# Norm statistics with tokens on partitions, one modulation slice ahead of the sums, GpSimd's sample tiles in another order, in a two-layer retention and attention trunk

## Chip, cores and metric

The kernel runs on one core of a Trainium2 chip. The metric is the device time of one execution in microseconds. A core has five engines that run side by side and meet at semaphores: TensorE (matrix products into PSUM), VectorE, ScalarE, GpSimd and SyncE, which here issues the loads of the weights.

## What is computed

Two layers of a hybrid encoder trunk, for a prompt (1 x 256 tokens) and for 8 sequences of 16 new tokens, 384 tokens in all, width 1024, fp32:

```python
mods = silu(c) @ w_ada + b_ada
sh1, sc1, g1, sh2, sc2, g2 = split(mods, 6)                 # per sequence
h  = rmsnorm(x, g_mix) * (1 + sc1) + sh1
u  = h @ w_in            # retention q, k, v, gate | attention q, k, v | two merge gates
x  = x + g1 * ((sig(m_r) * yA @ w_br_ret + sig(m_a) * yB @ w_br_att) @ w_out)
h2 = rmsnorm(x, g_ffn) * (1 + sc2) + sh2
x  = x + g2 * (relu(h2 @ w_up)**2 @ w_down)
rmsnorm(x, g) = x * rsqrt(mean(x * x over the 1024 features) + 1e-6) * g
```

yA is an eight-head retention, yB an attention over a band of chunks and a cache. The change is in `rmsnorm` and what stands around it.

## The kernel before

x is kept transposed, `xT[feature within tile, 8 feature tiles, 384 tokens]`: features lie on the partitions, so a sum over features is a sum across partitions, which TensorE does. Every large product is made of three passes on split operands (high times high, low times high, high times low; `hhi`/`hlo` for activations, `whi`/`wlo` for weights), and weight blocks of 128x1024 pass through four raw slots and two split slots: SyncE loads, ScalarE writes `whi` (`high`), VectorE writes `wlo` (`low`).

Each layer runs: norm, value product, eight heads, merge, output product, norm, up product, down product. The norm of layer 0's mixing takes its statistics from x before it is transposed (`first_tables`, `spread`) and isn't touched. The three others go through the same functions, and the order on each engine is written out by hand:

- ScalarE squares the feature tiles two at a time into `sq` (L802). GpSimd adds the first six into `sq_sum` (L430, L434); the last two stay in `sq`.
- TensorE, `norm` (L1635): with `ones` as the stationary operand it sums `sq_sum` (L1641) and the two `sq` tiles (L1644) over the partitions. Bank X0 then holds, on every partition, the sum of each of the 384 tokens.
- ScalarE, L815: square root of these 384 columns into `std`. VectorE, `inverse_std` (L1151): reciprocals of `std` into `rstd`, first the 128 sample columns (L1153), then the 256 prompt columns (L1154).
- Prompt part: VectorE scales tile k by `modA` and `rstd` into `hp` (L1164), ScalarE adds the shift and rounds into `hhi` (L827), VectorE forms `hlo` (L1169). Sample part: GpSimd, `norm_sample` (L637), multiplies by `modA` (L643), by `rstd` (L649) and adds the shift (L653); ScalarE rounds into `hhi` (L772), VectorE forms `hlo` (L1174). VectorE's order is `normed_tiles` (L1176): tile m's low parts come behind the scaling of tile m+2.
- TensorE meanwhile computes slices of the modulation (`silu(c) @ w_ada`, 512 columns each) for later use with stationary operands of 32 columns (L1650): `last_modulation` (L1833) in the norm ahead of the up product, three slices in layer 0 and two in layer 1, into X1, X2, X3; `ada_products` (L1655) in layer 1's mixing norm, the last of which writes X0.
- `steady` (L1877) and the end of `last_modulation` are dummies, products of `ones` with `ident` into a bank that nobody reads.
- The first product after the norm is `first_up` (L1847, matmuls on L1861) or the value product (L1627); each starts a tile when its `hlo` is there.

## Time and profile before

| | us |
|---|---|
| median of 3 runs | 1806.72 (1802.99 to 1807.86) |
| the profiled execution's own time | 1803.19 |
| its span | 1801.2 |
| TensorE busy in it | 1782.5 |
| VectorE, ScalarE, GpSimd busy | 994.8, 736.0, 353.4 |

The profiled execution lies 3.5 us below the median of the runs. Times in the rows are microseconds from the start of the span. A matmul on fp32 operands shows as two records, each with a weight load of its own (PEld); one on fp32r operands or a transpose shows as one. "x192" is a number of records merged into one row, whose time is from the first's start to the last's end.

### The profile page before, as it was taken

How to read it: one execution, taken by the hardware profiler on the slowest of the kernel's cores; microseconds unless marked ns; L12 is line 12 of the kernel's file. 1: busy time of each engine (PE TensorE's matmuls, PEld its weight loads, DVE VectorE, ACT ScalarE, POOL GpSimd, SP SyncE). 2: the span in 40 equal slices, each digit the busy share in tenths (PEclk: the TensorE clock that was granted, in tenths of full speed). 3: DMA queues.
4: the chain of work that ended last, by engine and by line, in shares of the span. 5: the costliest groups of instructions: out<-in, count | busy, mean ns of one | idle time of the engine just before them, and what ended most of it. 6: DMA issues, size and time to landing. Idle time of an engine off the chain costs nothing.

```text
span 1801.2 us, 35393 instructions
## 1 busy us (share of the span) xinstructions
PE 1782.5 (99%) x11933; PEld 1624.8 (90%) x11933; DVE 994.8 (55%) x1606; ACT 736.0 (41%) x1411; POOL 353.4 (20%) x459
## 2 busy tenths in 40 slices
PE   8999999999999999999999999999999999999998
PEld 7888888889999999999988888888899999999998
DVE  5466666667433575543364666666674346655333
ACT  3444444446222344532234444444463234554222
POOL 3333333330000120000023334333300004000000
PEclk9999999999999999999999999999999999999999
DMA  9878898896666734455638779888865635344432
GB/s 343 232 200 215 225 239 231 231 236 199 210 211 208 260 95 127 129 177 200 218 104 237 204 215 230 231 224 240 231 220 165 211 118 199 117 128 125 132 125 99
DMA packets 505240, 348.47 MB, mean 193 GB/s; under 512 B 201931, under 2 KB 468109, under 8 KB 505110
## 3 DMA queue, kind: packets, MB, share of 16 engines
q1 hardware_dynamic: 484992, 292.13, 56.3%
q0 software_dynamic: 12592, 44.99, 7.7%
q10 hardware_dynamic: 7526, 9.58, 1.5%
q8 instruction: 86, 1.41, 0.3%
q14 instruction: 44, 0.36, 0.1%
HBM read 313.56 MB, written 34.37 MB: 193 GB/s over the span
## 4 chain that ended last, share of the span: by engine, by line
PE 97%; DVE 1%; ACT 1%; issue 1%; ACTq 0%; POOL 0%; DVEq 0%
PE G L1591 50%; PE G L1627 32%; PE X L1752 8%; PE X L1650 2%; PE X L1551 2%; PE G L1861 2%; PE X L1627 1%; DVE wlo L1093 0%; PE X L1644 0%; DVE hp L1164 0%; DVE rstd L1154 0%; ACT hp L791 0%; ACTq L766 0%; ACT whi L772 0%; DVE hlo L1169 0%
## 5 line engine op out<-in xcount | busy, mean ns | idle before, releaser
L1093 DVE TENSOR_TENSOR wlo<-raw,whi 128x1024 fp32r<-128x1024 f32 x369 | 471.0, 1277 | 546.0 <-ACT whi L772 543.9
L772 ACT ACTIVATE whi<-raw 128x1024 fp32r<-128x1024 f32 x369 | 390.9, 1059 | 761.8 <-PE G L1591 442.3
L1627 PE MATMUL G<-whi,hhi 128*128 128x512 f32 x832 | 333.9, 401 | 1.7 <-DVE hlo L1169 1.4
L1627 PE MATMUL G<-whi,hlo 128*128 128x512 f32 x832 | 325.0, 391 | 0.0
L1627 PE MATMUL G<-wlo,hhi 128*128 128x512 f32 x832 | 324.5, 390 | 0.1
L1591 PE MATMUL G<-hhi,whi 128*128 128x384 f32 x704 | 236.8, 336 | 0.0
L1591 PE MATMUL G<-hhi,wlo 128*128 128x384 f32 x704 | 235.4, 334 | 0.0
L1591 PE MATMUL G<-hlo,whi 128*128 128x384 f32 x704 | 235.3, 334 | 0.0
L1627 PEld LDWEIGHTS G<-whi,hhi 128*128 128x128 f32 x832 | 156.2, 188 | 49.2 <-issue 13.1
L1591 PE MATMUL G<-ysp,whi 128*128 128x384 f32 x768 | 196.9, 337 | 0.0
L1627 PEld LDWEIGHTS G<-wlo,hhi 128*128 128x128 f32 x832 | 156.1, 188 | 34.1 <-DVE wlo L1093 0.6
L1627 PEld LDWEIGHTS G<-whi,hlo 128*128 128x128 f32 x832 | 156.4, 188 | 29.4
L1591 PE MATMUL G<-fhi,whi 128*128 128x384 f32 x512 | 172.5, 337 | 0.0
L1591 PE MATMUL G<-fhi,wlo 128*128 128x384 f32 x512 | 172.1, 336 | 0.0
L1591 PE MATMUL G<-flo,whi 128*128 128x384 f32 x512 | 172.1, 336 | 0.0
L1591 PEld LDWEIGHTS G<-ysp,whi 128*128 128x128 f32 x768 | 138.4, 188 | 1.5 <-issue 1.2
L1591 PEld LDWEIGHTS G<-hhi,whi 128*128 128x128 f32 x704 | 132.1, 188 | 2.8 <-issue 1.6
L430 POOL TENSOR_TENSOR sq_sum<-sq 128x384 f32<-128x384 f32 x4 | 5.1, 1286 | 655.4 <-ACT sq L802 655.4
L1591 PEld LDWEIGHTS G<-hlo,whi 128*128 128x128 f32 x704 | 132.2, 188 | 0.1
L1591 PEld LDWEIGHTS G<-hhi,wlo 128*128 128x128 f32 x704 | 132.1, 188 | 0.0
L1591 PE MATMUL G<-ysp,wlo 128*128 128x384 f32 x384 | 129.2, 336 | 0.0
L1591 PEld LDWEIGHTS G<-fhi,whi 128*128 128x128 f32 x512 | 96.1, 188 | 0.6 <-issue 0.6
(237 smaller groups left out, 2545.3 us busy)
## 6 DMA issues: line engine op xcount, KB each, us to landing
raw<-in_w_in_dram SPq DMA_DIRECT2D x256, 128.0 KB
raw<-in_w_in_dram SPq DMA_DIRECT2D x128, 256.0 KB
raw<-in_w_up_dram SPq DMA_DIRECT2D x64, 512.0 KB
raw<-in_w_down_dram SPq DMA_DIRECT2D x64, 512.0 KB
raw<-in_w_in_dram SPq DMA_DIRECT2D x49, 512.0 KB
ada_w<-in_w_ada_dram SPq DMA_DIRECT2D x44, 512.0 KB, 6.1
kc<-in_cache_attn_k_dram SPq DMA_DIRECT2D x64, 256.0 KB, 6.7
vc<-in_cache_attn_v_dram SPq DMA_DIRECT2D x32, 512.0 KB, 7.5
```

Source lines behind the costliest of these rows:

```text
L430: ops.tensor_tensor(sq_sum[:, :], sq[:, 0, :], sq[:, 1, :], ALU.add).then_inc(sq_used, 2)
L772: return a.activation(out, in_, ACT.Copy)
L1093: v.tensor_tensor(wlo[:, j % SPLIT, :, :], raw[:, j % RAW, :, :], whi[:, j % SPLIT, :, :].bitcast(F32), ALU.subtract).then_inc(blk_split, 1)
L1551: return t.transpose(out, in_, ident[0:k, 0:k])
L1591: ins = t.matmul(G[b][:, 0:TOK], w[:, s, k, n * P:(n + 1) * P], x[:, k0 + k, :], start=first and k == 0 and x is hi and w is whi, stop=las ...
L1627: ins = t.matmul(B[banks[m][0]][:, :], x[:, kp * WK + k, m * P:(m + 1) * P], w[:, k, :], start=first and k == 0 and x is hhi and w is w_hi ...
L1650: ins = t.matmul(x[32 * g:32 * g + 32, 0:P], cT[:, k, :], part, start=start, stop=stop, skip_group_check=True)
L1752: return t.matmul(out, lhsT, rhs, start=start, stop=stop, skip_group_check=True)
L1861: ins = t.matmul(G[b][:, 0:TOK], w[:, j % SPLIT, k % BK, n * P:(n + 1) * P], x[:, k, :], start=k == 0 and x is hhi and w is whi, stop=k == ...
```

## The change

It does five things. (1) In `norm` on TensorE the squares become the stationary operand and a column of `ones` the moving one: nine one-column matmuls put the sum of token p of tile n on partition p, column 384 + n, of X0; a tenth, over columns of `qr_par` that are always zero, opens the three columns. (2) ScalarE's root and VectorE's reciprocal work on three columns; VectorE lays the result out as three diagonal matrices (`std_diag`), TensorE multiplies them with `ones` (`std_spread`), which again puts each token's value on every partition, and VectorE copies X0 into `rstd`. (3) One slice of the modulation is issued ahead of `norm` instead of behind it, and in layer 1's mixing norm the remaining one waits for the copies out of X0. Layer 1 has four dummies fewer. (4) GpSimd multiplies four sample tiles by `modA` ahead of its wait for `rstd` and the other four between the later steps. (5) VectorE forms the first tile's low parts ahead of the third tile's scaling.

```diff
--- before.py
+++ after.py
@@ -223,7 +223,7 @@
     band = sb("band", [DEPTH * HEADS, BAND], stack=xstack)
     hp = sb("hp", [P, NS, PR], stack=xstack)
     hs = sb("hs", [P, KT, P], stack=xstack)
-    std = sb("std", [P, TOK], stack=xstack)
+    std_diag = sb("std_diag", [P, NT, P], stack=xstack)
     rstd = sb("rstd", [P, TOK], stack=xstack)
     x_diag = sb("x_diag", [P, NT, P], stack=xstack)
     x_ss = sb("x_ss", [P, 4], stack=xstack)
@@ -639,19 +639,38 @@
 
             pool.wait_ge(res_ready, c.norm * KT + R0)
             pool.wait_ge(moda_ready, c.norm * 4 + 4)
-            for k in range(KT):
+            scaled, normal = {}, {}
+
+            def scale(k):
                 c.op(g.tensor_tensor(seqs(hs[:, k, :]), seqs(xT[:, k, PR:TOK]),
                                      modA[:, k, 1:NSEQ].unsqueeze(2).to_broadcast([P, SB, ST]), ALU.mult))
-            c.settle()
+                scaled[k] = c.now["own"] + c.mine
+
+            def normalize(k):
+                pool.wait_ge(pool_own, scaled[k])
+                c.op(g.tensor_tensor(hs[:, k, :], hs[:, k, :], rstd[:, PR:TOK], ALU.mult))
+                normal[k] = c.now["own"] + c.mine
+
+            def shifted(k):
+                pool.wait_ge(pool_own, normal[k])
+                d = seqs(hs[:, k, :])
+                g.tensor_tensor(d, d, modT[:, shift * KT + k, 1:NSEQ].unsqueeze(2).to_broadcast([P, SB, ST]),
+                                ALU.add).then_inc(hs_ready, 1)
+
+            for k in range(KT // 2):
+                scale(k)
             pool.wait_ge(rstd_ready, c.norm * 2 + 1)
-            for k in range(KT + 1):
-                if k < KT:
-                    c.op(g.tensor_tensor(hs[:, k, :], hs[:, k, :], rstd[:, PR:TOK], ALU.mult))
-                if k:
-                    pool.wait_ge(pool_own, c.now["own"] + (c.mine - 1 if k < KT else c.mine))
-                    d = seqs(hs[:, k - 1, :])
-                    g.tensor_tensor(d, d, modT[:, shift * KT + k - 1, 1:NSEQ].unsqueeze(2).to_broadcast([P, SB, ST]),
-                                    ALU.add).then_inc(hs_ready, 1)
+            normalize(0)
+            shifted(0)
+            normalize(1)
+            for k in range(KT // 2, KT):
+                scale(k)
+                shifted(k - 3)
+                normalize(k - 2)
+            for k in range(KT - 3, KT - 1):
+                shifted(k)
+                normalize(k + 1)
+            shifted(KT - 1)
 
         def store_prompt_state(c, l, h):
             pool.wait_ge(stp_ev, c.head)
@@ -812,7 +831,7 @@
                 high(c, 1)
                 square(c, KT - 2)
                 act.wait_ge(sq_used, c.norm * KT + KT)
-                a.activation(std[:, :], X[0][:, 0:TOK], ACT.Sqrt, scale=1.0 / DM, bias=eps_t[:, 0:1]).then_inc(std_ready, 1)
+                a.activation(rstd[:, 0:NT], X[0][:, TOK:TOK + NT], ACT.Sqrt, scale=1.0 / DM, bias=eps_t[:, 0:1]).then_inc(std_ready, 1)
             for k in range(KT):
                 if first and k in (2, 4, 6):
                     if k > 2:
@@ -1150,8 +1169,13 @@
 
         def inverse_std(c):
             dve.wait_ge(std_ready, c.norm + 1)
-            v.reciprocal(rstd[:, PR:TOK], std[:, PR:TOK]).then_inc(rstd_ready, 1)
-            v.reciprocal(rstd[:, 0:PR], std[:, 0:PR]).then_inc(rstd_ready, 1)
+            c.op(v.reciprocal(rstd[:, 4:4 + NT], rstd[:, 0:NT]))
+            c.settle()
+            v.tensor_tensor(std_diag[:, :, :], ident[:, :].unsqueeze(1).to_broadcast([P, NT, P]),
+                            rstd[:, 4:4 + NT].unsqueeze(2).to_broadcast([P, NT, P]), ALU.mult).then_inc(diag_ready, 1)
+            dve.wait_ge(spread_done, c.norm + 1)
+            v.tensor_copy(rstd[:, PR:TOK], X[0][:, PR:TOK]).then_inc(rstd_ready, 1)
+            v.tensor_copy(rstd[:, 0:PR], X[0][:, 0:PR]).then_inc(rstd_ready, 1)
 
         def modulated(c, shift, gain, k0, k1):
 
@@ -1175,20 +1199,24 @@
 
         def normed_tiles(c, shift, k0, k1, block=None, at=None, free=None):
 
+            def tile_low(m):
+                dve.wait_ge(hhi_ready, c.norm * KT + (m + 1))
+                if m == k0 and free is not None:
+                    dve.wait_ge(ada_used, free)
+                c.op(sample_low(m))
+                prompt_low(shift, m).then_inc(h_ready, 1)
+
             for k in range(k0, k1 + 2):
                 if k == (k1 if at is None else at) and block is not None:
                     low(c, block)
+                if k == k0 + 2:
+                    tile_low(k0)
                 if k < k1:
                     if k >= NS:
                         dve.wait_ge(h_ready, c.norm * KT + (k - NS + 1 + H0))
                     scaled(k)
-                if k >= k0 + 2:
-                    m = k - 2
-                    dve.wait_ge(hhi_ready, c.norm * KT + (m + 1))
-                    if m == k0 and free is not None:
-                        dve.wait_ge(ada_used, free)
-                    c.op(sample_low(m))
-                    prompt_low(shift, m).then_inc(h_ready, 1)
+                if k > k0 + 2:
+                    tile_low(k - 2)
 
         def first_modulation(c, part):
 
@@ -1635,13 +1663,24 @@
         def norm(c):
 
 
-            pe.wait_ge(std_ready, c.norm)
+            pe.wait_ge(rstd_ready, c.norm * 2)
             pe.wait_ge(pair_ev, c.head * 4 + P0)
             pe.wait_ge(sq_used, c.norm * KT + KT - 2)
-            t.matmul(X[0][:, 0:TOK], ones[:, :], sq_sum[:, :], start=True, stop=False)
-            for n in range(2):
-                pe.wait_ge(sq_ready, c.norm * KT + (KT - 1 + n))
-                t.matmul(X[0][:, 0:TOK], ones[:, :], sq[:, n, :], start=False, stop=(n == 1)).then_inc(sq_used, 1)
+            mm(X[0][:, TOK:TOK + NT], ones[:, :], qr_par[:, 0, ST:ST + NT], stop=False)
+            for n in range(NT):
+                mm(X[0][:, TOK + n:TOK + n + 1], sq_sum[:, n * P:(n + 1) * P], ones[:, 0:1], start=False, stop=False)
+            for k in range(2):
+                pe.wait_ge(sq_ready, c.norm * KT + (KT - 1 + k))
+                for n in range(NT):
+                    ins = mm(X[0][:, TOK + n:TOK + n + 1], sq[:, k, n * P:(n + 1) * P], ones[:, 0:1], start=False, stop=(k == 1))
+                ins.then_inc(sq_used, 1)
+
+        def std_spread(c):
+
+            pe.wait_ge(diag_ready, c.norm + 1)
+            for n in range(NT):
+                ins = mm(X[0][:, n * P:(n + 1) * P], ones[:, :], std_diag[:, n, :])
+            ins.then_inc(spread_done, 1)
 
         def ada_product(x, k, w, start, stop, blocks=True):
 
@@ -1830,15 +1869,12 @@
                         ada_products(mixed(l, 20 * i + j))
                         j += 1
 
-        def last_modulation(l):
-
-            for f in range(ADA_F + 1 - l):
-                pe.wait_ge(adaf_full[f], l * 32 + 32)
-                for k in range(KT):
-                    ins = ada_product(X[1 + f], k, adaf_w[:, f, k, :], k == 0, k == KT - 1)
-                ins.then_inc(ada_mm, 1)
-            for _ in range(8 * l):
-                mm(X[3][:, 0:P], ones[:, :], ident[:, :])
+        def last_modulation(l, f):
+
+            pe.wait_ge(adaf_full[f], l * 32 + 32)
+            for k in range(KT):
+                ins = ada_product(X[1 + f], k, adaf_w[:, f, k, :], k == 0, k == KT - 1)
+            ins.then_inc(ada_mm, 1)
 
         def up(c):
             for j in range(4):
@@ -1911,9 +1947,10 @@
         for l in range(DEPTH):
             if l:
                 with cnt.turn({"norm": 1}, use=("norm", "head")) as c:
+                    ada_products(ADA_GAP)
                     norm(c)
-                    ada_products(ADA_GAP)
-                    pe.wait_ge(std_ready, c.norm + 1)
+                    std_spread(c)
+                    pe.wait_ge(rstd_ready, c.norm * 2 + 2)
                     ada_products(ADA_GAP + 1)
                 steady(4)
             with cnt.turn(S_V.adds, also=("norm",)) as c:
@@ -1936,8 +1973,14 @@
                     pe.wait_ge(m_ready, c.mix + j % 2 * BK)
                     products(c, S_OUT, j, S_OUT.groups[j // 2], mhi, mlo, j % 2 * BK, j % 2 == 0, j % 2 == 1)
             with cnt.turn({"norm": 1}, use=("norm", "head")) as c:
+                pe.wait_ge(pair_ev, c.head * 4 + P0)
+                last_modulation(l, 0)
                 norm(c)
-            last_modulation(l)
+                std_spread(c)
+            for f in range(1, ADA_F + 1 - l):
+                last_modulation(l, f)
+            for _ in range(4 * l):
+                mm(X[3][:, 0:P], ones[:, :], ident[:, :])
             with cnt.turn(S_UP0.adds, also=("norm",)) as c:
                 first_up(c)
             with pe.Fori(0, S_UP.turns - 1) as i, cnt.turn(S_UP.adds) as c:
```

## Rows read from the trace of the kernel before

**Rows 1.** The page's first part: busy time, share of the span, instructions.
```profile
PE 1782.5 (99%) x11933; PEld 1624.8 (90%) x11933; DVE 994.8 (55%) x1606; ACT 736.0 (41%) x1411; POOL 353.4 (20%) x459
```

**Rows 2.** What TensorE waited for: total us, times, longest.
```profile
PE X L1644 <- ACT sq L802: 2.7, 3, 0.9
...
PE G L1861 <- DVE wlo L1093: 0.8, 2, 0.4
```

**Rows 3.** The chain that ended last, layer 0, feed-forward norm: start, us, what.
```profile
629.95 1.57 PE X L1644 x4
...
631.55 0.59 ACT std L815
...
634.87 0.48 DVE hp L1164
...
636.57 0.49 DVE hlo L1174
```

**Rows 4.** Timeline of the same norm: start, us, engine, line, [idle before, releaser].
```profile
628.23 0.81 PE L1641 MATMUL X<-sq_sum,ones 128*128 128x384 f32 x2
...
629.39 1.05 ACT L802 ACTIVATE sq<-xT 128x384 f32<-128x384 f32 x2
...
631.44 5.45 PE L1650 MATMUL X<-adaf_w,cT 128*32 128x128 f32 x192
...
635.95 0.29 ACT L772 ACTIVATE hhi<-hs 128x128 fp32r<-128x128 f32 x1
...
637.71 0.45 PE L1861 MATMUL G<-hhi,whi 128*128 128x384 f32 x1 [0.82 <-DVE hlo L1169]
```

**Rows 5.** Timeline of layer 1's mixing norm, TensorE.
```profile
912.02 0.81 PE L1641 MATMUL X<-sq_sum,ones 128*128 128x384 f32 x2
...
918.86 1.16 PE L1752 MATMUL X<-ident,ones 128*128 128x128 f32 x8
...
921.40 0.50 PE L1627 MATMUL G<-whi,hhi 128*128 128x512 f32 x1 [1.38 <-DVE hlo L1169]
```

**Rows 6.** Timeline of layer 1's feed-forward norm, TensorE.
```profile
1516.15 0.81 PE L1641 MATMUL X<-sq_sum,ones 128*128 128x384 f32 x2
...
1525.60 0.44 PE L1861 MATMUL G<-hhi,whi 128*128 128x384 f32 x1 [0.56 <-DVE hlo L1169]
```

**Rows 7.** Loads of `adaf_w`, both layers: ns of issue, first and last start.
```profile
L543 SPq DMA_DIRECT2D adaf_w<-in_w_ada_dram x8: 372/490/1223, 597.4 to 1494.5; - x8
...
DMA to landing us min/median/max: 5.1/9.2/12.1
```

**Rows 8.** Timeline of the program's start, TensorE: narrow transposes, dummies.
```profile
9.97 0.66 PE L1551 MATMUL G<-ident,csil 9*128 9x9 f32 x8 [0.43 <-ACT csil L795]
...
20.21 1.06 PE L1752 MATMUL X<-ident,ones 128*128 128x128 f32 x8
```

**Rows 9.** Weight loads by line, min/median/max ns, first and last start.
```profile
L1551 PEld LDWEIGHTS G<-ident,csil x8: 133/136/138, 10.0 to 10.4; 9*128 9x128 f32 x8
...
L1641 PEld LDWEIGHTS X<-sq_sum,ones x6: 188/188/189, 628.1 to 1516.1; 128*128 128x128 f32 x6
...
L1650 PEld LDWEIGHTS X<-adaf_w,cT x320: 106/110/110, 631.4 to 1522.7; 128*32 128x32 f32 x160
```

**Rows 10.** Small operations: timeline rows, then groups (busy us, mean ns of one).
```profile
626.64 0.20 ACT L811 ACTIVATE warm<-eps_t 128x1 f32<-128x1 f32 x1
...
13.40 0.56 DVE L1124 TENSOR_TENSOR x_diag<-ident,x_rs 128x384 f32<-128x384 f32 x1 [0.35 <-POOL x_rs L613]
...
L1387 DVE RECIPROCAL small<-small 128x3 f32<-128x3 f32 x16 | 2.7, 168 | 0.0
...
L1145 DVE COPY ada_s<-X 128x128 f32<-128x128 f32 x20 | 5.7, 283 | 0.0
...
L649 POOL TENSOR_TENSOR hs<-hs,rstd 128x128 f32<-128x128 f32 x24 | 13.2, 555 | 0.5 <-POOL hs L643 0.5
```

**Rows 11.** Stretches: us, busy (instructions) by engine, granted clock, DMA share, GB/s.
```profile
12.10:19.00 6.90, 6.23 (x65) 5.52 (x67) 1.93 (x7) 2.21 (x4) 2.45 (x4) 0.51 1.08 366
...
912.00:921.40 9.40, 7.11 (x145) 5.29 (x143) 7.77 (x13) 4.48 (x10) 7.58 (x16) 1.00 0.34 108
```

## The prediction

> **What bounds the kernel now.** I read the page first. TensorE is busy 99% of the span [rows 1]. So only two things can move the end: TensorE's own work, and the few places where it stands still. The list of what TensorE waited for [rows 2] and the timeline [rows 4 to 6] name them. Apart from the start of the program the largest are the squares of the last two feature tiles (2.7 us in three waits) and the first normalized tile (0.82 and 0.56 us before the two up products, 1.38 us before the value product). All lie in the three norms that the change edits: feed-forward norm of layer 0 (A), mixing norm of layer 1 (B), feed-forward norm of layer 1 (C). The norm of layer 0's mixing is a separate code path and is not touched.
>
> The chain of waits through A gives the anatomy [rows 3]. The sums end at 631.5; I call this moment T, where bank X0 holds the sums. Then ScalarE takes the root of 384 columns (0.59), VectorE inverts as many, the first scaled tile starts at 634.87 = T+3.36, and TensorE's first real product starts at 637.71 [rows 4], 2.84 us after that. Meanwhile TensorE does something useful: 192 records of three modulation slices, 5.45 us [rows 4], so one slice (64 records) is 1.82 us. The whole stop from 628.23 to 637.71 is 9.5 us, and B (912.02 to 921.40) and C (1516.15 to 1525.60) are 9.4 and 9.5 us [rows 5, 6]. In A the old sums' first record starts at 628.23, 3.28 before T; B and C have the same steps, so T is 915.3 and 1519.43 there.
>
> **Part 1, the slice in front of the sums.** In A and C one of the modulation slices, in B the slice that stood between the sums and the wait for the root, is issued before the sums. The work is the same, 1.82 us; it fills the time in which TensorE waited for the squares. Its weights landed long before: the latest of the loads named in [rows 7] is issued at 1494.5, over 21 us ahead of the sums in C, and lands within 12.1; in A and B they are earlier still. A change from products over all 128 columns to slices over 32 costs about 0.2 us: the dummies start 0.2 us after the last slice record [rows 5]. In A the slice runs from 628.43 to 630.25 and the sums may start at 630.45. The last square is finished at 630.44 (629.39 plus 1.05) [rows 4]. So until here nothing is lost: TensorE arrives just as the data does. But nothing of the sums has been done by then either, whereas before the part over `sq_sum` was already finished (628.23 plus 0.81). All ten matmuls of the new sums now stand behind T's last input.
>
> **Part 2, the sums with tokens on partitions.** Before: three matmuls of 384 columns, two records each. After: ten matmuls (one that opens three columns, three over `sq_sum`, two times three over `sq`), each with a new 128x128 fp32 stationary operand and one to three moving columns, 20 records. Moving columns cost nothing; the weight load is what is left. The trace of before has no such matmul, so I bound it. From below: eight transposes of 9 rows, one record each, take 0.66 us in all, 0.202 the last, so 0.065 apart [rows 8]. From above: dummies of 128 fp32 columns, 8 records in 1.06 us, 0.113 apart [rows 8]. Between them decides the duration of a load: 0.188 for 128 columns of fp32, 0.110 for 32 columns, 0.136 for the 9-row transposes [rows 9]. 96 more columns cost 0.078 us, so 128 columns occupy the load path for 0.104 us, and a load that isn't a transpose costs more than the transposes' one. I take 0.11 per record: 0.1 for the first load, 19 x 0.11 and 0.2 for the last matmul, 2.39 us. New T in A is 630.45 + 2.39 = 632.84, 1.33 later than before. In B: 912.2 + 1.82 + 0.2 + 2.39 = 916.6 against 915.3. In C: 1516.35 + 1.82 + 0.2 + 2.39 = 1520.76 against 1519.43. With 0.065 per record the sums take 1.54 and T is 0.45 to 0.5 later.
>
> The Trainium skill prices this otherwise: its page "TensorEngine Tiling (Array Packing)", section "Instruction Overhead", gives each matmul about 60 cycles of overhead whatever its few columns, which at 2.4 GHz is an estimated 25 ns. By that alone the 20 records would take 0.5 us and the whole change would come out at about 2.3 us faster. The load rows above speak against it, since none of them is that short for 128 columns.
>
> **Part 3, root, inverse and spreading.** From T on: ScalarE starts 0.04 later, root of three columns 0.2 (a one-column ScalarE instruction [rows 10]); VectorE inverts three columns in 0.168 [rows 10], hand-overs 0.02 before and 0.15 after it; `std_diag` is the same instruction as `x_diag` at the program's start, 0.56 [rows 10]; TensorE starts 0.05 later and spreads with six records: 5 x 0.113 + 0.27 = 0.84; VectorE copies 128 and 256 columns out, 0.1 + 0.28 [rows 10] + about 0.35 = 0.73; 0.13 to the first scaled tile. Sum 2.89 against 3.36: 0.47 saved. The wait for the spread stands in VectorE's queue; behind it are only the copies and the scaled tiles, which need it anyway. GpSimd waits for the same sum.
>
> **Part 4, order of the tiles.** VectorE takes the low part of the first tile before it scales the third. Before, the third scaled tile kept it until 636.57 although ScalarE had the sample part at 635.95 + 0.29 = 636.24 [rows 3, 4]: 0.27 gained. First tile ready to TensorE: T + 2.89 + 2.84 - 0.27 = T+5.46. The second tile then comes 0.5 us later relative to the first (two scaled tiles in front), about 2.1 us behind it, which is what TensorE needs for one tile's six matmuls over both groups (12 x 0.17): no stall. GpSimd's new order does tile 0 first and puts the four remaining modulated copies between the others: at some 0.55 us per instruction [rows 10] tile 1 is ready at T+5.1, tile 3 at T+8.2, before VectorE comes to them (its own pace is 1.55 us per tile). No cost, no gain.
>
> **Part 5, TensorE's own path after the spread.** The spread's last record is issued at T+1.76, the next slice may start at about T+2.0. A: two slices 3.63 + 0.2: first product at T+5.83, later than the tile (T+5.46), so TensorE's work decides. A = 632.84 + 5.83 = 638.67, against 637.71: **+0.96**. C: one slice and four dummies (fewer by four, 0.9 us less work) end near T+4.9, so the tile decides: 1520.76 + 5.46 = 1526.22 against 1525.60: **+0.62**. B: here the remaining slice writes X0 and now waits for both copies out of it, T+2.76: 2.81 + 1.79 + 0.2 + four dummies 0.95 = T+5.75, so the work decides: 916.61 + 5.75 = 922.36 against 921.40: **+0.96**. Sum +2.5 us. With the lower price of the sums it is +0.1, +0.1 and -0.2, together 0.0.
>
> What is late next: nothing else moves with it. In A and C a wait of 0.4 us for the low half of the third weight block follows eight steps later; that block waits for TensorE to free a slot, so the wait travels along.
>
> **The forecast.** Against the profiled execution's own time, 1803.19 (span 1801.2 and 2.0 around it), +2.5 gives 1805.7. The three runs shown have a median of 1806.72 and lie between 1802.99 and 1807.86; on the median's footing it is **1809.2 us**. About 0.3% (5.4 us) is what a measurement of this kernel can tell from no change, so this is no change.
>
> **Rivals.** (1) *Narrow matmuls are cheap.* At 0.065 per record the sum is 0.0: 1806.7. For it: the transposes. Against: the load rows. (2) *The clock falls*, the slower case. Before, the granted clock is full through all three norms, yet near the start it fell to half (1.2 of 2.4 GHz) at about 12.1 and stayed there until about 19, after a spell of eight 9-column transposes with gaps on either side [rows 8, 11]. That is like the new stretch: 2.4 us of one-column matmuls, then 1.2 us of standing still for the root and the diagonal, before only half such gaps. Price: of 6.85 us at half clock some 1.5 are waits anyway, the other 5.35 lose half, 2.7 us per norm. One fall gives 1806.7 + 2.5 + 2.7 = 1811.9, all three 1817.3. It decides from two falls on (1814.6), and one lies at the border of 0.3%. The page "TensorE: Matmul & The Clock Gate" of the Trainium skill, section "A second HAM failure mode: psum-queue depth-cycling", says that short idle times between groups of matmuls are enough to make the clock swing; by it this rival would be the rule, though the gaps of 0.9 and 0.8 us in the norms of before did not do it. Against it too: slices and dummies stand on both sides. (3) *A gain*: loads go in ahead under the slice, and little is left after the last square. Then T is up to 0.1 earlier than before, TensorE's path T+5.8 against 6.2, about -0.8 per norm: 1804.3, still within 0.3%. More than 5.4 us can't come out: it would take 1.8 us per norm, and TensorE's slices, spread and dummies leave no such room.
>
> **How the numbers follow.** Forecast 0.55, narrow matmuls cheap 0.20, clock 0.17, gain 0.08. The range takes in the gain with some spread of the runs below it, and one or two falls above: 1803.5 to 1814.5. Faster by over 0.3%: 0.02; slower: 0.14, nearly all of the clock rival; same 0.84.
>
> **What would show it.** In the changed profile: starts of the one-column records 0.11 apart and the span from the last square to the root's start near 2.4 us; the first scaled tile 2.9 us behind the root's start; in A and B no wait between the last slice or dummy and the first product, in C one; the low part of tile 0 ahead of the third scaled tile; the granted clock at 1.00 in the three stretches. The prediction is wrong if records stand 0.06 apart or less, if a spread takes twice 0.84, or if TensorE waits inside the up product for tiles 1 to 3.

## The result and the profile after

The changed kernel takes 1811.04 us, the median of eight runs (1808.27 to 1812.92), against 1803.93 for the kernel before in eight runs (1802.09 to 1807.86). The ratio is 1.0034, with a 95% interval of [1.0023, 1.0045]: it is slower by 7.1 us. The range of the prediction (1803.5 to 1814.5) holds the 1811.04, but its likeliest case ("no change", +2.5 us) did not come. The profiled execution took 1812.92 us.

The page's first part; the row that answers to it is [rows 1]:

```profile
PE 1790.5 (99%) x11985; PEld 1633.8 (90%) x11985; DVE 990.4 (55%) x1612; ACT 733.2 (40%) x1411; POOL 352.5 (19%) x459
```

TensorE is busy 8.0 us longer. The 52 more records are three times 20 for the sums and 6 for the spread, less three times 6 of the old sums and 8 of the dummies, and few of them are long. So the same work must in part have taken longer. What TensorE waited for (total us, times, longest), to be held against [rows 2]:

```profile
PE X L1791 <- DVE std_diag L1174: 3.5, 3, 1.2
...
PE G L1655 <- DVE wlo L1112: 1.4, 3, 1.0
...
PE G L1897 <- DVE wlo L1112: 0.8, 2, 0.4
PE X L1689 <- DVE rstd L1178: 0.7, 1, 0.7
```

The waits for the squares and for the first tile's low half have gone from the up products. In their place stand three waits for `std_diag` and one for the copies. Now norm A on the timeline, beside [rows 4]:

```profile
628.71 1.95 PE L1689 MATMUL X<-adaf_w,cT 128*32 128x128 f32 x64
...
631.51 1.48 PE L1791 MATMUL X<-ones,sq 128*128 128x1 f32 x12
...
633.53 0.56 DVE L1174 TENSOR_TENSOR std_diag<-ident,rstd 128x384 f32<-128x384 f32 x1
...
634.15 1.65 PE L1791 MATMUL X<-std_diag,ones 128*128 128x128 f32 x6 [1.16 <-DVE std_diag L1174]
...
635.73 4.58 PE L1689 MATMUL X<-adaf_w,cT 128*32 128x128 f32 x128
...
640.23 0.45 PE L1897 MATMUL G<-hhi,whi 128*128 128x384 f32 x1
```

The one-column sums are as dear as forecast. But the spread's six records take 1.65 us where 0.84 was forecast, and the 128 records of two slices 4.58 where the sum had 3.63. The stretches of the changed kernel (columns as in [rows 11]; the granted clock is the number before the last two) say why:

```profile
630.00:632.50 2.50, 2.50 (x43) 2.30 (x34) 1.64 (x3) 0.82 (x2) 1.80 (x3) 1.00 0.17 57
632.50:634.20 1.70, 0.54 (x6) 0.46 (x5) 0.73 (x2) 0.26 (x1) 0.60 (x2) 0.99 0.47 133
634.20:637.60 3.40, 3.40 (x42) 3.05 (x46) 1.63 (x4) 0.48 (x2) 1.24 (x3) 0.50 0.25 88
637.60:640.00 2.40, 2.40 (x96) 2.40 (x92) 2.17 (x6) 1.42 (x5) 2.40 (x5) 1.00 0.04 10
920.90:927.70 6.80, 6.08 (x76) 5.18 (x75) 3.82 (x9) 1.97 (x6) 6.09 (x14) 0.50 0.01 2
1528.50:1535.20 6.70, 5.65 (x72) 4.82 (x73) 4.32 (x11) 2.10 (x6) 3.44 (x8) 0.50 0.26 80
1528.50:1529.50 1.00, 0.00 (x0) 0.00 (x0) 0.73 (x2) 0.20 (x1) 0.00 (x1) 0.50 0.73 174
```

In A the clock is full until the end of the gap (the wait for `std_diag`), falls to half (1.2 of 2.4 GHz) as the spread begins, and comes back 3.4 us later. It falls in B and C too, for 6.8 us each, but not at the same place: in B towards the end of the spread (920.9), in C right behind the last record of the sums (they end at 1528.40), so that the whole gap of C passes at half clock already. In the kernel before it stayed at 1.00 in B's stop [rows 11], and in A's and C's too.

That the profiled execution is no exception shows in the mean granted clock of every execution: 0.993 to 0.997 in the eight of the changed kernel, and the four at 0.993 and 0.994 are its four longest (1811.15 to 1812.92 us). The kernel before has 0.997 to 1.000 in 85 of its 87 executions beside the experiments; the other two took 2205 and 2526 us at 0.752 and 0.654 and enter no ratio.

In what follows a norm's *stop* is the time from the last large product to the start of the next one: it begins 0.17 us after the last record's start, which is the distance at which another such record would have followed. *Through* means from the same beginning to the last record of the first up product, again plus 0.17, and so takes in the waits inside it. From the timelines, in us:

| kernel | stop A | stop B | stop C | A through | C through | norms in which the clock falls |
|---|---|---|---|---|---|---|
| before | 9.49 | 9.38 | 9.46 | 26.92 | 26.90 | none |
| changed | 11.61 | 12.49 | 11.86 | 29.06 | 29.26 | A, B, C |
| changed, profiled again (e10) | 11.69 | 11.65 | 12.07 | 29.11 | 29.49 | A, B, C |
| sums with 128 columns (e2 below) | 10.13 | 10.32 | 9.52 | 27.69 | 27.67 | none |
| the same, profiled again (e11) | 10.13 | 10.32 | 9.52 | 27.68 | 27.70 | none |

The profile's span is 10.2 us longer than before's; the three stops are 7.6 of it. 2.2 lie between B's stop and C's, and these are not the change's: in e10, the same kernel profiled again, that distance is the one of before to 0.4 us. The 7.1 us of the medians are about the stops.

### The profile page after: what moved, and what is told of

The parts are those of the page before. It is cut to its first block, busy times and chain, and to the rows that moved or that the text cites. A ratio compares the mean times of both kernels' runs of the same rounds, so it can differ in the third digit from the quotient of the medians.

```text
span 1811.4 us, 35533 instructions
## 1 busy us (share of the span) xinstructions
PE 1790.5 (99%) x11985; PEld 1633.8 (90%) x11985; DVE 990.4 (55%) x1612; ACT 733.2 (40%) x1411; POOL 352.5 (19%) x459
## 4 chain that ended last, share of the span: by engine, by line
PE 87%; SPq 7%; issue 2%; DMA 1%; DVE 1%; ACT 1%; POOL 0%; DVEq 0%; ACTq 0%
PE G L1619 50%; PE G L1655 24%; PE X L1791 7%; PE X L1689 2%; SPq L453 2%; SPq L500 2%; PE G L1897 2%; PE X L1579 2%; DMA raw<-in_w_in_dram 1%; SPq L380 1%; SPq L474 1%; PE X L1655 1%; DVE wlo L1112 1%; ACT whi L791 1%; SPq L462 0%
```

## The experiments

All ratios are against the kernel before on the same chip; the medians stand beside it. Three theories were put against each other. *Clock:* the extra time is the clock that falls, and it falls because of the gap, of the one-column sums, or of both. *Sums:* the one-column sums and the spread cost more than the sum had. *Waits:* a late tile or a wait that took the removed one's place. The quoted expectations use letters: K is the clock theory, S the loss by structure (sums and waits), N that the one-column records bring the clock down, G that standing still does.

### e1_gap_filled

The changed kernel, and TensorE computes dummies while it would wait for `std_diag` (in all three norms):

```diff
                 norm(c)
+                steady(5)
                 std_spread(c)
```

> The changed kernel with five dummies (ones times ident, as in steady) between the sums and the wait for the diagonal, in all three norms; they are about 1.2 us of work and the wait is 1.16 to 1.24 us, so the path gets no longer. Theory K (the clock's fall during the spread and the slices behind it costs some 5 us of the 7, the longer path of the sums the other 2.5): the granted clock stays at 1.00 in all three norms, the spread takes 0.85 to 0.95, the time is 2 to 3 us above the kernel before, 1806 to 1807. Rival S (the loss is in structure: 20 records behind the last square, the wait for the copies out of X0, loads that are disturbed; the clock is incidental): 1810 to 1811 as without dummies. Rival N (it is the stretch of one-column records before the gap that makes the clock fall, not the standing still): the clock falls all the same, 1810 or more.

1811.71 against 1804.36, 1.0040 [1.0026, 1.0054]. The gap is closed and the clock falls in A and C all the same, in B it does not. Theory K expected 1806 to 1807 with a full clock and is refuted in this form; rival N stands. TensorE's timeline in A (this profile's A begins 4.7 us later in the program):

```profile
638.90 1.54 PE L1791 MATMUL X<-std_diag,ones 128*128 128x128 f32 x6
```

The stretches of A (three rows), C and B of the same kernel:

```profile
629.00:639.00 10.00, 10.00 (x122) 9.43 (x120) 5.60 (x11) 4.81 (x7) 3.24 (x5) 1.00 0.45 133
639.10:642.40 3.30, 3.30 (x46) 2.94 (x49) 1.65 (x4) 0.63 (x3) 1.38 (x3) 0.50 0.24 82
636.00:644.00 8.00, 8.00 (x128) 7.51 (x131) 4.38 (x11) 1.73 (x6) 4.84 (x10) 0.79 0.23 70
1529.00:1535.00 6.00, 6.00 (x88) 5.54 (x87) 2.39 (x6) 0.98 (x4) 2.27 (x6) 0.72 0.30 90
920.00:932.00 12.00, 11.29 (x174) 9.89 (x163) 7.78 (x19) 4.32 (x12) 7.97 (x16) 1.00 0.22 73
```

In A TensorE is busy for 10.00 of 10.00 us at full clock, and then the clock falls, with 8.00 of 8.00 us busy around it and 0.79 granted on average. So standing still is not needed for a fall. This profile has one more fall, from 232.9 to 239.7 among layer 0's heads, where the code is that of before and no other profile here has one. What set it off is open; it is part of why this A begins later.

### e2_wide_columns

The changed kernel, but the sums' moving operand is `ones` with 128 columns instead of one. The records and weight loads are as many as before, the sum of a token stands in 128 columns, and the root reads the first of each block:

```diff
-                mm(X[0][:, TOK + n:TOK + n + 1], sq_sum[:, n * P:(n + 1) * P], ones[:, 0:1], start=False, stop=False)
+                mm(X[0][:, n * P:(n + 1) * P], sq_sum[:, n * P:(n + 1) * P], ones[:, :], start=False, stop=False)
...
-                    ins = mm(X[0][:, TOK + n:TOK + n + 1], sq[:, k, n * P:(n + 1) * P], ones[:, 0:1], start=False, stop=(k == 1))
+                    ins = mm(X[0][:, n * P:(n + 1) * P], sq[:, k, n * P:(n + 1) * P], ones[:, :], start=False, stop=(k == 1))
```

> The changed kernel with the sums' moving operand 128 columns of ones instead of one (nine products of 128x128 by 128 columns; every column of a block holds the same sums, ScalarE's root reads one column of each block). The records' pace stays at 0.115, since the weight load sets it. The gap of 1.2 us before the spread stays. Rival N (one-column records bring the clock down): the granted clock stays at 1.00 in the norms, 1806 to 1807. Theory G (the standing still brings it down): it falls as before, 1810 to 1811. If both share, it falls in some norms or some executions: 1808 to 1809.

1806.70 against 1804.36, 1.0018 [1.0003, 1.0032]. Norm C on this kernel's timeline:

```profile
1520.22 1.50 PE L1791 MATMUL X<-ones,sq 128*128 128x128 f32 x12
1521.77 0.26 ACT L834 ACTIVATE rstd<-X,eps_t 128x3 f32<-128x3 f32 x1 [2.30 <-PE X L1791]
...
1522.88 0.94 PE L1791 MATMUL X<-std_diag,ones 128*128 128x128 f32 x6 [1.16 <-DVE std_diag L1174]
...
1524.62 1.03 DVE L1188 SCALAR_TENSOR_TENSOR hp<-xT,modA,rstd 128x256 f32<-128x256 f32 x2
...
1526.77 0.45 PE L1897 MATMUL G<-hhi,whi 128*128 128x384 f32 x1
```

Its three norms' stretches:

```profile
628.00:640.00 12.00, 10.84 (x217) 10.13 (x208) 8.63 (x19) 4.29 (x11) 8.04 (x15) 1.00 0.24 76
912.00:924.00 12.00, 10.13 (x170) 8.86 (x171) 7.64 (x17) 4.68 (x11) 7.44 (x15) 1.00 0.25 82
1518.00:1530.00 12.00, 10.84 (x164) 9.90 (x157) 8.63 (x19) 4.32 (x11) 8.02 (x15) 1.00 0.23 73
```

Twelve records of 128 moving columns take 1.50 us, those of one column 1.48: the columns are nearly free, as the prediction had it. Over all 20 records it is 2.49 us here (1519.23 to 1521.72) and 2.39 in the changed kernel's A (630.60 to 632.99). The gap is still there (1.16), and the clock stays full in all three norms. This one kernel shows both things: that the clock does not fall here with wide columns in the same records, and what the change costs without the falls. The medians alone would not carry this, since the intervals of e2 and of the changed kernel overlap (up to 1.0032, from 1.0023). The clocks of the executions do: ten of e2's eleven have 0.998 to 1.000, against 0.993 to 0.997; the eleventh has 0.996 and took 1815.84 us, and what happened in it no profile shows.

### e3_slice_behind

The changed kernel with part 1 undone, the slice behind sums and spread:

```diff
-                pe.wait_ge(pair_ev, c.head * 4 + P0)
-                last_modulation(l, 0)
                 norm(c)
                 std_spread(c)
-            for f in range(1, ADA_F + 1 - l):
+            for f in range(ADA_F + 1 - l):
```

> The changed kernel with the modulation slice back behind the sums and the spread (part one undone). The sums over sq_sum now run while TensorE waits for the squares, so the root starts about 1.3 us earlier after the last square than with the slice in front, 1.0 instead of 2.3 us behind it. But TensorE has 1.8 us more to do after the spread, which decides in all three norms: by my steps the same end within 0.5 us in each. With its gaps (0.9 before the squares and 1.2 before the spread) the clock should fall at least as often: theory K 1810 to 1813. Rival S, if the slice in front was the culprit: 1805 to 1806.

1813.10 against 1804.36, 1.0049 [1.0035, 1.0063]; stops 13.38, 11.90, 12.40. The clock falls in all three norms, in A and C before the gap, within the one-column sums. C's sums on the timeline:

```profile
1525.73 2.29 PE L1791 MATMUL X<-ones,sq 128*128 128x1 f32 x12 [0.78 <-ACT sq L821]
```

The stretch in A behind 631.50:

```profile
631.50:634.00 2.50, 1.22 (x9) 1.13 (x8) 1.74 (x3) 0.26 (x1) 2.16 (x4) 0.59 0.14 24
```

The same twelve records take 2.29 us instead of 1.48. With the slice in front the stops were 11.61 and 11.69 in A, 11.86 and 12.07 in C (the two profiles of the changed kernel): 1.7 us less in A and 0.4 in C. In B (12.49 and 11.65) the two profiles differ by more than they do from e3. These differences are not the slice's alone: the fall in A lasts 6.8 us here (632.0 to 638.8) and 3.4 in the changed kernel. The rival that the slice in front was the culprit (1805 to 1806) is refuted.

### e4_slice_in_gap

The changed kernel with the slice between the one-column sums and the spread, in the place of the gap:

```diff
-                last_modulation(l, 0)
                 norm(c)
+                last_modulation(l, 0)
                 std_spread(c)
```

> The changed kernel with the slice between the sums and the spread instead of in front of the sums. TensorE's 1.8 us of slice cover the wait for the diagonal (1.2 us), so no gap is left there, and the root starts 1.3 us earlier. Theory K: clock at 1.00, the first product within 0.3 us of the kernel before in each norm, together 1804 to 1805 (+0 to +1). Rival S: 1808 or more, since the 20 records and the wait for X0 are still there.

1806.23 against 1804.36, 1.0016 [1.0005, 1.0027]; stops 9.54, 11.03, 8.93. The clock stays full in A and C and falls in B, at 915.9, inside the slice that fills the gap:

```profile
912.00:924.00 12.00, 10.51 (x165) 9.13 (x165) 7.10 (x16) 4.21 (x11) 7.01 (x14) 0.86 0.24 77
915.90:919.30 3.40, 2.93 (x34) 2.25 (x26) 0.54 (x3) 0.00 (x0) 0.00 (x0) 0.50 0.39 140
```

One-column sums alone don't bring it down every time: with a slice of 1.8 us right behind them it fell once in three in this profile. In e1 the place was filled too, with ten records instead of 64, and it fell twice. How often it falls differs between executions of the same kernel: seven of e4's eleven have a granted clock of 0.998 and take 1804.3 to 1808.5 us, the other four have 0.993 to 0.997 and take 1808.4 to 1811.5. Theory K, which expected a full clock in every norm and 1804 to 1805, held in two norms of three.

### e5_tile_order_only

The kernel before with part 4's order of VectorE's tiles and nothing else:

```diff
             for k in range(k0, k1 + 2):
+                if k == k0 + 2:
+                    tile_low(k0)
                 if k < k1:
...
                     scaled(k)
-                if k >= k0 + 2:
+                if k > k0 + 2:
+                    tile_low(k - 2)
```

> The kernel before with VectorE's new tile order alone (the first tile's low parts ahead of the third tile's scaling). In all three norms the first product waited for the first tile, so each stop gets shorter by the 0.27 us that the third scaled tile cost: 9.2, 9.1 and 9.2 us instead of 9.5, 9.4 and 9.5, together 0.8 us, 1803.6 against 1804.4; too little for the runs to tell, so it is read from the stops. If the second tile is late instead (0.5 us behind), the up product waits inside and the gain is gone.

1804.41 against 1803.29, 0.9997 [0.9987, 1.0008]. Nothing that the medians can tell, but the stops are 8.93, 8.89 and 8.92: 0.5 less in each norm, where the prediction had 0.27. C on the timeline:

```profile
1525.28 0.29 DVE L1174 TENSOR_TENSOR hlo<-hs,hhi 128x128 fp32r<-128x128 f32 x1 [0.23 <-ACT hhi L772]
...
1526.17 0.45 PE L1865 MATMUL G<-hhi,whi 128*128 128x384 f32 x1
```

The sample low part takes 0.29 us here, in the old order it took 0.49 [rows 3]. These 0.2 us and the forecast 0.27 make up the 0.5. Why it is shorter in the new place no run separates. Through the first up product A and C are 0.4 us shorter each (26.50 and 26.52), so most of the gain is kept.

### e6_before_no_dummies and e9_before_narrow_dummies

Two kernels that leave the new sums out altogether. e6 is the kernel before without its four dummies in B and eight in C:

```diff
-                steady(4)
...
-            for _ in range(8 * l):
-                mm(X[3][:, 0:P], ones[:, :], ident[:, :])
```

> The kernel before without its four and eight dummies in layer 1's two norms. TensorE then stands still before the first product for some 2.5 us in each of them, with no one-column record anywhere. If standing still alone brings the clock down (theory G), it falls here in one or both norms or in the first products: 1806 to 1808. If it takes the one-column records (theory N), the granted clock stays at 1.00 and the time at that of before, 1804, since the dummies stood beside the chain.

1806.03 against 1803.29, 1.0013 [1.0004, 1.0022]. The stops are as long as before (9.46, 9.38, 9.45), but TensorE now stands still for 2.5 us in B and in C (2.46 and 2.54), and behind that the clock falls, for 3.4 us each (from 921.6 and 1529.2). The value product's start on the timeline:

```profile
920.74 0.50 PE L1627 MATMUL G<-whi,hhi 128*128 128x512 f32 x1 [2.46 <-DVE hlo L1169]
```

The stretches of B and C:

```profile
912.00:926.00 14.00, 10.62 (x149) 8.30 (x149) 10.90 (x18) 4.75 (x12) 11.77 (x24) 0.88 0.20 61
1518.00:1534.00 16.00, 12.55 (x164) 10.85 (x163) 14.08 (x26) 7.62 (x18) 12.14 (x24) 0.89 0.23 68
```

e9 keeps these dummies, each with one moving column instead of 128 (the same weight loads):

```diff
-                mm(X[3][:, 0:P], ones[:, :], ident[:, :])
+                mm(X[3][:, 0:1], ones[:, :], ident[:, 0:1])
```

> The kernel before with its four and eight dummies of layer 1's norms kept, but with one moving column instead of 128: the same number of 128-column weight loads, at the same pace, in the same places. If one-column records keep the engine's clock up as the full ones do, nothing changes: granted clock 1.00 in both norms, 1803.5 to 1804.5. If they count for nothing (theory N), the kernel behaves as the one without any dummies: the clock falls in one or both of layer 1's norms, while the stops stay at 9.4 and 9.5, and the time is 1805.5 to 1807.

1807.48 against 1804.56, 1.0014 [1.0003, 1.0025]; stops 9.47, 9.37, 9.46. B's dummies and its first product on the timeline:

```profile
917.82 0.70 PE L1752 MATMUL X<-ident,ones 128*128 128x1 f32 x5
...
919.99 0.80 PE L1627 MATMUL G<-whi,hhi 128*128 128x512 f32 x1 [1.47 <-DVE hlo L1169]
```

The stretches of B and C:

```profile
912.00:926.00 14.00, 12.18 (x160) 9.97 (x161) 10.18 (x17) 4.18 (x12) 11.76 (x24) 0.88 0.15 42
1518.00:1534.00 16.00, 14.43 (x180) 12.71 (x179) 14.55 (x27) 7.62 (x18) 12.13 (x24) 0.89 0.21 65
```

The wait ahead of the product is 1.47 us, nearly the 1.38 of the kernel before [rows 5], and the dummies' weight loads are all there; still the clock falls in both norms for 3.4 us, as it does without any dummies. In these two profiles one-column dummies did for the clock what no dummies do. The price shows behind the stop: C through the first up product takes 28.5 us in e6 and 28.4 in e9, against 26.90 before. This is the reading of e2 from the other side, in a kernel with the old sums.

### e7_wide_slice_in_gap, e8_wide_gap_no_dummies

e7 joins e2 and e4: 128 moving columns, slice in the gap.

```diff
-                last_modulation(l, 0)
                 norm(c)
+                last_modulation(l, 0)
                 std_spread(c)
...
+                mm(X[0][:, n * P:(n + 1) * P], sq_sum[:, n * P:(n + 1) * P], ones[:, :], start=False, stop=False)
```

> The slice between the sums and the spread, and 128 moving columns in the sums. Theory N: the granted clock is 1.00 in all norms of every profile (with one column it still fell in the mixing norm of layer 1). Stops by the profile of the one-column version where its clock held: 9.5 in A, 8.9 in C, and in B 11.0 less the 1.2 us that the half clock cost, 9.8: together 28.3, the same as before; 1804.0 to 1804.8.

1804.62 against 1803.29, 1.0014 [1.0003, 1.0024]; stops 9.64, 9.83, 9.03, no fall in the profile (of the other ten executions one, of 1812.06 us, has a granted clock of 0.996, the rest 0.998 to 1.000). e8 is e7 without its dummies in B and C:

```diff
-                steady(4)
...
-            for _ in range(4 * l):
-                mm(X[3][:, 0:P], ones[:, :], ident[:, :])
```

> The same, and no dummies in layer 1's norms. In B TensorE's own work (slice into X0 behind the copies, then four dummies) sets the end; without the dummies the tile sets it: stop 9.4 instead of 9.8. C is set by the tile, 8.9. Together 27.8 against 28.3 of before: 1803.5 to 1804.2. If standing still brings the clock down, C and B pay it back.

1804.40 against 1803.29, 1.0008 [0.9999, 1.0017]; stops 9.64, 9.82, 9.02, no fall. With the slice in the gap and full columns the dummies are not needed to hold the clock. B's stop was expected to shrink to 9.4 and did not. Without the dummies TensorE waits for the first tile in B and in C, and the stops are those of e7 to 0.01 us:

```profile
921.36 0.50 PE L1655 MATMUL G<-whi,hhi 128*128 128x512 f32 x1 [1.08 <-DVE hlo L1193]
1526.48 0.44 PE L1897 MATMUL G<-hhi,whi 128*128 128x384 f32 x1 [1.06 <-DVE hlo L1193]
```

So the dummies only filled the time up to the tile. Neither kernel is faster than the one before.

### e10_changed_second_look, e11_wide_second_look

The changed kernel and e2 once more, one execution each, to see whether the falls repeat.

> The changed kernel, profiled a second time, since where the clock falls may differ between executions. Theory K: it falls in at least two of the three norms again, and a stop without a fall is 10.1 (A), 10.3 (B) or 9.5 (C), as with the wide columns.

> The changed kernel with 128 moving columns in the sums, profiled a second time. Theory N: granted clock 1.00 in all three norms again. If the gap of 1.2 us has a part of its own in the fall, it shows in one of them.

They do: 1809.19 us with falls in A, B and C (3.4, 3.4 and 6.8 us; in C it comes 0.5 us into the gap, at 1524.9), against 1804.35 us with none, and 1804.56 for the kernel before. The stops stand in the table above.

### e12_old_gpsimd_order

e7 with GpSimd's order of before, in short:

```diff
-            for k in range(KT // 2):
+            for k in range(KT):
                 scale(k)
             pool.wait_ge(rstd_ready, c.norm * 2 + 1)
...
-                scale(k)
-                shifted(k - 3)
-                normalize(k - 2)
```

In e7, as in e2, a wait for `wlo` inside C's up product was 1.1 us where before has 0.4. The chain of it in C on e2's timeline:

```profile
1533.35 0.47 POOL L657 TENSOR_TENSOR hs<-hs,modT 128x128 f32<-128x128 f32 x1
1533.85 0.31 ACT L791 ACTIVATE hhi<-hs 128x128 fp32r<-128x128 f32 x1 [0.30 <-POOL hs L657]
1534.07 1.05 ACT L791 ACTIVATE whi<-raw 128x1024 fp32r<-128x1024 f32 x1
1535.14 1.23 DVE L1112 TENSOR_TENSOR wlo<-raw,whi 128x1024 fp32r<-128x1024 f32 x1
```

The chain reads: GpSimd hands over a late sample tile; ScalarE waits for it; the weight block's high half stands behind that in ScalarE's queue; VectorE's low half follows, and TensorE waits for it.

> Wide columns and slice in the gap as in the earlier kernel of that kind, with GpSimd's sample tiles in the order of before (eight modulated copies ahead of the wait, then two steps per tile). Theory P: the new order delays the last sample tiles, ScalarE's whi of the third weight block stands behind them in its queue, and so in layer 1's feed-forward norm (C) the up product waits 1.1 us for wlo where it waited 0.4 before. Then the wait is 0.4 to 0.6 here, and from the end of the output product to the end of the first up product C takes 26.6 to 26.8 us instead of 27.2 (before: 26.9). In A little changes (0.5 us of waiting before, at most 0.1 less). The first product may be up to 0.2 us later, since GpSimd has four more copies ahead of the first tile. Rival: the wait comes from the product's earlier start and VectorE's own pace; then it stays at 1.1. Time: 1804 either way, within what runs can tell.

1804.66 against 1805.59, 1.0000 [0.9990, 1.0009]. The wait is back at 0.40, and C through the first up product takes 26.89 instead of 27.21, a little above the expected 26.6 to 26.8. But its stop grew from 9.03 to 9.31, with a wait for the first tile's sample part that e7 did not have:

```profile
1528.15 0.45 PE L1878 MATMUL G<-hhi,whi 128*128 128x384 f32 x1 [0.26 <-DVE hlo L1174]
```

So the new GpSimd order hands over the first tile earlier and the last ones later. In C the two together were worth 0.3 us against it, in A 0.1; in B, whose stop grew from 9.83 to 10.03, the new order is worth 0.2 us.

## Why the prediction came out as it did

**The likeliest case was wrong by the clock, and by little else in the sum.** With full clock (e2 and e11) the three norms are +0.77, +0.94 and +0.77 us longer than before, taken through the first up product in A and C and as the stop in B: +2.5, the forecast sum, and e2's medians are +2.3 apart. What stands between e2 and the changed kernel in the same places is 1.4 in A (29.06 less 27.69), 1.6 in C, 2.2 in B: 5.2 us. 2.5 and 5.2 make 7.7, the medians show 7.1; with e10's norms it is 4.6 instead of 5.2, and together 7.1.

**That the range holds the result is partly luck.** Its upper end, 1814.5, was meant for one or two falls on a kernel before of 1806.7. There were three, at less than the price forecast, and the kernel before had a median of 1803.93 in eight runs instead of 1806.72 in three. On that footing the forecast of +2.5 is 1806.4. Two of the prediction's own signs came out against it: the granted clock is not 1.00 in the three stretches, and the spread takes 1.65 us in A and C, nearly twice 0.84.

**Part 1** held. TensorE arrived with the squares: there is no wait between the slice and the sums, and in A the root starts 4.4 us after the stop's beginning, where the forecast's sum had 4.6. The new sums end 1.1 to 1.2 us later in the stop than the old ones did, the forecast was 1.33. e3 puts a price on the slice's place only together with the clock.

**Part 2**, price of a record: forecast 0.11 us, measured 0.115 from start to start, 20 records in 2.34 us on the chain of waits through A:

```profile
630.67 2.34 PE X L1791 x20
633.00 0.02 issue
633.03 0.27 ACT rstd L834
...
634.15 1.65 PE X L1791 x6
635.80 4.51 PE X L1689 x128
```

The rival of cheap narrow matmuls (0.065) has fallen, and with it the reading of the page "TensorEngine Tiling (Array Packing)" of the Trainium skill, section "Instruction Overhead", by which 20 records would be 0.5 us: for matmuls that each bring 128 new columns of weights the trace disagrees nearly fivefold. Setting the price by the load rows and not by the transposes was the right choice.

**Part 3**: forecast T+2.89 for the first scaled tile, measured 2.89 in e2's C (1521.73 to 1524.62). The terms compensate: the root 0.26 instead of 0.2, the spread 0.94 instead of 0.84, a little less in the hand-overs and copies.

**Part 4** has a mis-sized term and a missed one. The tile order brought 0.5 us per norm instead of 0.27 (e5): the forecast counted the delay by the third scaled tile and not the low part's own 0.2 us. GpSimd's new order brings the first tile forward too, by up to 0.3 us (e12: C's stop 9.31 against 9.03), where the forecast had nothing. In C, where the tile was to decide, the stop without falls is thus +0.06, not +0.62. But "no cost, no gain" for GpSimd's order and "the wait travels along" for the wait inside the up product were wrong in C: 0.41 became 1.10, 0.7 us, and e12 shows GpSimd's order as the cause. I had compared the time at which each sample tile is ready with VectorE's pace alone. ScalarE's queue, in which a weight block stands behind a sample tile, was not looked at. The misses, 0.56 us in the stop and 0.7 behind it, are opposite, which is why C came out at +0.77 and near the forecast. In the changed kernel itself the falls hide the second one: TensorE comes later, and the wait is 0.40.

**Part 5**, without the falls: in A TensorE's own work decides, as forecast. In C the first tile decides, as forecast too, though TensorE's matmul row shows no wait. The tile comes so much earlier that the dummies just reach up to it, and the wait stands only in the row of the first product's weight load, in e2's C:

```profile
1526.77 0.19 PEld L1897 LDWEIGHTS G<-hhi,whi 128*128 128x128 f32 x1 [0.17 <-DVE hlo L1193]
```

B is the step that was read wrongly. Its +0.94 matches the forecast +0.96, but the dummies in that sum don't decide: in e8 they are gone and the stop is the same, with 1.08 us of waiting for `hlo`. VectorE forms the first low part only when the slice into X0 is done (in e8 it waits 0.97 us for that slice and starts at 920.42), and that part and the prompt's low part behind it take about as long as the dummies. In the changed kernel itself the falls stretch TensorE's work, and it decides in C as well.

**Rival 2, the clock.** Mechanism and sign were right, also that it decides from two falls on; its chance of 0.17 was too low. The step that failed in the likeliest case is the argument against this rival, "slices and dummies stand on both sides": both profiles of the changed kernel fall in A, B and C, six of six. The price was off too: 2.7 us per norm were taken from a fall of 6.85 us as at the program's start. In A it lasted 3.4 us and cost 1.4; in B and C it lasted 6.8, as forecast, but cost 2.2 and 1.6. At three falls the rival said 1817.3 and the kernel shows 1811.0. Of these 6.3 us 2.8 are the footing and 2.9 the price of the falls (8.1 against 5.2).

What sets it off is shown in part. Shown: with 128 moving columns in the same matmuls and the same gap it didn't fall (e2, e11; six norms). One-column dummies did nothing to hold it (e9 against e6, one profile each). A wait of 2.5 us without any one-column record ahead of it also brings it down (e6), while 1.4 us didn't before [rows 5]. The gap is not needed (e1 in two of three norms, e3 during the sums, and the changed kernel's C, where the clock is at half as the gap begins). The changed kernel takes full-width work away twice, in the sums and in the gap, and it had been near the edge: the kernel before holds its clock in B and C only by its dummies. Open: how much of a fall in the changed kernel is due to the gap and how much to the sums, why e4 fell in B and not in A or C, e1 in A and C and not in B, and why a fall lasts 3.4 us in one execution and 6.8 in another (B: 6.8 and 3.4). The section "A second HAM failure mode: psum-queue depth-cycling" of the page "TensorE: Matmul & The Clock Gate" of the Trainium skill blames short idle times between groups of matmuls. These runs agree only by half: e1 fell without idle time, e2 held with 1.16 us of it.

**No version beats the kernel before by more than the medians can tell.** Nearest are e5 (0.9997; its norms are 1.3 us shorter together by the profile) and e12 (1.0000). The gain that the new norm promised was a shorter way from T to the first tile (0.47 by the root, spread and copies, 0.5 by the tile order); the sums give back 1.1 us per norm, since all of them stand behind the last square (root's start 4.4 us into the stop, before 3.3).

## What to carry to other kernels

A matmul with few moving columns and a new 128-column fp32 stationary operand is priced by its weight load: count records times their distance (here 0.115 us), not columns. On a kernel that TensorE bounds, look at the granted clock of every stretch in which you replace wide matmuls by narrow ones or by a wait, and don't rely on the narrow ones to hold it; making the moving operand wide again cost 0.1 us per norm (stops 9.64 and 9.03 in e7, 9.54 and 8.93 in e4) and kept the clock in all profiles. A stop that matches a forecast sum need not be set by the terms of that sum; taking the dummies out (e8) showed what sets it. And when an engine's order is changed, follow each handed-over tile into the next engine's queue, to what stands behind it there, and not only to its consumer.

## What the runs showed of the hardware

- Records of a one-column matmul and of a 128-column one take nearly the same time with fp32 operands of 128 stationary columns: 1.48 and 1.50 us for twelve, 2.39 and 2.49 us for the 20 of a norm.
- TensorE that shows as busy can lose its clock: 8.00 of 8.00 us busy at 0.79 granted in e1, behind 10.00 of 10.00 us busy at 1.00, and within a row of one-column records in e3 (twelve in 2.29 us instead of 1.48).
- Eight fp32 dummy records of 128 columns in B and sixteen in C, in time that would be idle anyway, are what keeps the clock at 2.4 GHz through layer 1's norms of the kernel before. Without them (e6) the clock falls in both, and the time is 1.0013 [1.0004, 1.0022] of before, at unchanged stops.
- In the changed kernel a fall lasted 3.4 or 6.8 us. It cost 1.3 to 1.4 us at 3.4 and 1.6 to 2.2 at 6.8 (both profiles), less than half its length. Part of a fall lies on time in which TensorE waits: 0.7 us of B's and 1.1 of C's.
- The same kernel falls in one execution and not in another: e4's eleven have mean granted clocks from 0.993 to 0.998.
